# Stick-breaking attention: score banks in a ring of three pieces, turned weights in a ring of four

## What is computed

```python
def sb_attend(q, q_pos, k, v, k_pos):
    z = einsum('bqhd,bkhd->bhqk', q, k) * (SB_HEAD_DIM ** -0.5)
    mask = (k_pos[None, :] < q_pos[:, None])[None, None]
    log_keep = where(mask, log_sigmoid(-z), 0.0)
    suffix = cumsum(log_keep, axis=3, reverse=True) - log_keep
    a = where(mask, exp(log_sigmoid(z) + suffix), 0.0)
    return einsum('bhqk,bkhd->bqhd', a, v)
```

## Time and profile before

| | |
|---|---|
| median of three runs | 3169.32 us |
| the profiled execution, its time | 3168.51 us |
| its span, first to last instruction | 3166.7 us |
| PE busy, share of the span | 2966.6 us, 94% |
| PEld | 2641.9 us, 83% |
| DVE | 1229.3 us, 39% |
| ACT | 973.0 us, 31% |
| POOL | 631.6 us, 20% |
| mean granted clock of PE | 0.975 |

### The profile page before, as it was taken

One profiled execution on the slowest core, in us unless ns is written; L12 is line 12 of the kernel. 1 busy time (PEld: TensorE's weight loads), 2 busy tenths in 40 slices (PEclk: granted clock), 3 DMA queues, 4 the chain that ended last, 5 costly groups with the idle time before them and its releaser, 6 DMA issues. The chain is left out here.

```text
span 3166.7 us, 43362 instructions
## 1 busy us (share of the span) xinstructions
PE 2966.6 (94%) x16067; PEld 2641.9 (83%) x16067; DVE 1229.3 (39%) x1881; ACT 973.0 (31%) x1875; POOL 631.6 (20%) x484
## 2 busy tenths in 40 slices
PE   7989996999999999998999898898799999999998
PEld 6778885788899988997988677777679998899987
DVE  5556651432233322334111265667333332233324
ACT  4344443231122111223222365656322221122212
POOL 3100000121122111211212144444112211122111
PEclk9989997999999999999999999999899999999999
DMA  4211103310111111111355553633401111111111
GB/s 145 79 43 40 41 29 122 135 47 27 39 53 53 40 27 39 53 40 69 122 158 178 167 126 86 135 93 71 142 7 54 53 46 33 38 41 53 46 34 73
DMA packets 216172, 227.81 MB, mean 72 GB/s; under 512 B 50688, under 2 KB 174080, under 8 KB 216064
## 3 DMA queue, kind: packets, MB, share of 16 engines
q1 hardware_dynamic: 216064, 226.41, 24.3%
HBM read 170.36 MB, written 56.00 MB: 71 GB/s over the span
## 5 line engine op out<-in xcount | busy, mean ns | idle before, releaser
L1449 DVE TENSOR_TENSOR x<-m_ps,x 128x512 f32<-128x512 f32 x324 | 224.1, 692 | 669.7 <-PE m_ps L76 669.7
L1484 DVE TENSOR_TENSOR m_sq<-m_relu 128x384 f32<-128x384 f32 x192 | 171.9, 895 | 526.4 <-ACT m_relu L1388 526.4
L74 PE MATMUL m_ps<-h_h,m_up0h 128*128 128x384 f32 x768 | 259.0, 337 | 8.1 <-POOL m_up0l L1422 8.1
L75 PE MATMUL m_ps<-h_l,m_up0h 128*128 128x384 f32 x768 | 258.5, 337 | 0.0
L76 PE MATMUL m_ps<-h_h,m_up0l 128*128 128x384 f32 x768 | 258.5, 337 | 0.0
L74 PE MATMUL m_ps<-h_h,m_up1h 128*128 128x384 f32 x768 | 256.5, 334 | 0.0
L75 PE MATMUL m_ps<-h_l,m_up1h 128*128 128x384 f32 x768 | 256.5, 334 | 0.0
L76 PE MATMUL m_ps<-h_h,m_up1l 128*128 128x384 f32 x768 | 256.5, 334 | 0.0
L1388 ACT ACTIVATE m_relu<-m_ps 128x384 f32<-128x384 f32 x192 | 94.6, 492 | 515.8 <-PE m_ps L76 515.7
L2170 POOL TENSOR_TENSOR e_b<-e_b,e_r 128x128 f32<-128x128 f32 (+7 forms) x128 | 155.1, 1216 | 235.5 <-DVE e_r L2216 228.1
L2216 DVE TENSOR_TENSOR_SCAN e_r<-e_ps,e_zero 128x128 f32<-128x128 f32 (+7 forms) x128 | 173.1, 1352 | 49.8 <-ACT e_ps L2083 43.0
(11 more groups left out here) (510 smaller groups left out, 7612.6 us busy)
## 6 DMA issues: line engine op xcount, KB each, us to landing
m_up_raw<-in_mlp_w_up SPq DMA_DIRECT2D x64, 512.0 KB, 4.6
m_dn_raw<-in_mlp_w_down SPq DMA_DIRECT2D x64, 512.0 KB, 3.6
h_raw<-scratch_oT SPq DMA_DIRECT2D x4, 1536.0 KB, 15.8
scratch_qr<-a_qrst SPq DMA_DIRECT2D x9, 512.0 KB, 3.4
a_x<-in_x_prompt SPq DMA_DIRECT2D x8, 512.0 KB, 4.8
b_qr<-scratch_qr SPq DMA_DIRECT2D x4, 1024.0 KB, 6.6
scratch_oT<-b_o SPq DMA_DIRECT2D x32, 128.0 KB, 1.7
new_p_sb_k<-d_rows SPq DMA_DIRECT2D x16, 256.0 KB, 2.0
```

What stands on the lines that cost most here:

```text
L74: pe.matmul(out, w[0], m[0], start=start, stop=False)
L75: pe.matmul(out, w[0], m[1], start=False, stop=False)
L1449: dve.tensor_tensor(x[:, t, cols], bank[:, 4 + n % 3, :], x[:, t, cols], ALU.add).then_inc(added.sem, 1)
L1484: dve.tensor_tensor(sq[n % 2][:], relu[n % 2][:], relu[n % 2][:], ALU.mult).then_inc(sq_done.sem, 1)
```

## The change

Scores, sigmoids and scan of a step go by pieces of at most one bank. `chunks` gives a step's pieces, the one with the last keys first: one piece up to 512 keys; for 640 keys 256 and then 384, for 768 keys 256 and 512, for 896 keys 384 and 512, for 1024 keys 512 and 512. Banks 0 to 2 hold the pieces in a ring of three, so a piece waits for the scan of the piece three before it. The scan of a second piece starts from the last value of the first, which it waits for. Semaphores `e_s`, `e_kept`, `e_taken` and `e_scan` count pieces where they counted steps. POOL's product still covers a whole step. The bank set free goes to the transposes and the sample: their ring has four banks, 3 to 6.

```diff
--- before.py
+++ after.py
@@ -1874,6 +1874,19 @@
         return n // SbSchedule.PAIR_STEPS % 2, m // 2 % 2, 2 * (m // 4) + m % 2
 
     @classmethod
+    def chunks(cls, n):
+
+
+        keys = max((cls.where(n)[2] + 1) * P, 2 * P)
+        ends = [0, keys - 2 * P if keys == 5 * P else 4 * P, keys] if keys > 4 * P else [0, keys]
+        return [(a, b - a) for a, b in zip(ends, ends[1:])][::-1]
+
+    @classmethod
+    def chunks_before(cls, n):
+
+        return sum(len(cls.chunks(m)) for m in range(n))
+
+    @classmethod
     def sample_task(cls, n):
 
         if n % 2 == 0:
@@ -1958,12 +1971,12 @@
         wT = sb("e_wT", [P, 2, P])
         o_smp = sb("e_osmp", [P, S.PAIRS, DEC_BATCH, DEC_SEQ])
         bank = ctx.enter_context(nc.psum_tensor("e_ps", [P, 8, 512], F32))
-        score = [bank[:, 2 * u:2 * u + 2, :].rearrange("p b c -> p (b c)") for u in range(2)]
+        CHUNKS = S.chunks_before(S.STEPS)
 
         qk_in, v_in = signal("e_qk_in"), signal("e_v_in")
         s_done = signal("e_s")
         kept, taken = signal("e_kept"), signal("e_taken")
-        scanned, weighted = signal("e_scan", 2), signal("e_weighted", 2)
+        scanned, weighted = signal("e_scan", 3), signal("e_weighted", 2)
         t_done, t_hi, t_lo = signal("e_t"), signal("e_t_hi"), signal("e_t_lo", 3)
         pv_done, o_done = signal("e_pv", 2), signal("e_o", 1)
         ck_in, cv_in = signal("e_ck_in"), signal("e_cv_in")
@@ -1974,13 +1987,19 @@
         const_done = signal("e_const")
         o_out = [signal(f"e_o_out{u}", 16) for u in range(2)]
 
+        def pieces(n):
+
+            used = (S.where(n)[2] + 1) * P
+            c = S.chunks_before(n)
+            return [(c + j, key, min(width, used - key), bank[:, (c + j) % 3, 0:width])
+                    for j, (key, width) in enumerate(S.chunks(n))]
+
         def slot(m):
 
-            m %= TASKS
-            return m % 3 if m < TASKS - 1 else 1
+            return m % 4
 
         def task_bank(m):
-            return bank[:, 4 + slot(m), :]
+            return bank[:, 3 + slot(m), :]
 
         def emptied(pe, i, m):
 
@@ -2045,7 +2064,7 @@
                             load_cache_v(i, 1, 2 * i + 1)
                         if g == 0 and not (last and pair == 1):
 
-                            s_done.wait(sp, S.STEPS * i + S.PAIR_STEPS * pair)
+                            s_done.wait(sp, CHUNKS * i + CHUNKS // 2 * pair)
                             load_queries_keys(sp, scratch, operands[1 - pair], 2 * i + pair + 1, qk_in.sem)
                             pv_done.wait(sp, S.UNITS * i + S.UNITS // 2 * pair)
                             load_values(sp, scratch, operands[1 - pair], 2 * i + pair + 1, v_in.sem)
@@ -2073,14 +2092,14 @@
 
             def weights(i, n):
 
-                first, _, used = score_columns(S.where(n)[2])
-                z = score[n % 2][:, first:first + used]
-                s_done.wait(act, S.STEPS * i + n + 1)
                 if n >= 4:
 
                     t_done.wait(act, TASKS * i + S.before(n - 3))
-                act.activation(take[n % 4][:, 0:used], z, ACT.Sigmoid, scale=SB_SCALE).then_inc(taken.sem, 1)
-                act.activation(z, z, ACT.Sigmoid, scale=-SB_SCALE).then_inc(kept.sem, 1)
+                for c, key, used, z in pieces(n):
+                    s_done.wait(act, CHUNKS * i + c + 1)
+                    act.activation(take[n % 4][:, key:key + used], z[:, 0:used], ACT.Sigmoid,
+                                   scale=SB_SCALE).then_inc(taken.sem, 1)
+                    act.activation(z[:, 0:used], z[:, 0:used], ACT.Sigmoid, scale=-SB_SCALE).then_inc(kept.sem, 1)
 
             def sample(i, kind, f, ps):
                 if kind == "keys":
@@ -2164,8 +2183,8 @@
             def weigh(i, n):
 
                 used = (S.where(n)[2] + 1) * P
-                scanned.wait(pool, S.STEPS * i + n + 1)
-                taken.wait(pool, S.STEPS * i + n + 1)
+                scanned.wait(pool, CHUNKS * i + S.chunks_before(n + 1))
+                taken.wait(pool, CHUNKS * i + S.chunks_before(n + 1))
                 b = take[n % 4][:, 0:used]
                 pool.tensor_tensor(b, b, rest[n % 2][:, SEQ - used + 1:SEQ + 1], ALU.mult).then_inc(
                     weighted.sem, 1)
@@ -2209,13 +2228,17 @@
             const_done.wait(dve, 12)
 
             def scan(i, n):
-                first, _, used = score_columns(S.where(n)[2])
-                keep = score[n % 2][:, first:first + used]
-                kept.wait(dve, S.STEPS * i + n + 1)
+                total = (S.where(n)[2] + 1) * P
                 weighted.wait(dve, S.STEPS * i + n - 1)
-                dve.tensor_tensor_scan(rest[n % 2][:, SEQ - used:SEQ][:, ::-1], keep[:, ::-1],
-                                       zero[:].broadcast_to([P, used]), 1.0, ALU.mult, ALU.add).then_inc(
-                                           scanned.sem, 1)
+                for c, key, used, keep in pieces(n):
+                    kept.wait(dve, CHUNKS * i + c + 1)
+                    at, start = SEQ - total + key, 1.0
+                    if key + used < total:
+                        scanned.wait(dve, CHUNKS * i + c)
+                        start = rest[n % 2][:, at + used:at + used + 1]
+                    dve.tensor_tensor_scan(rest[n % 2][:, at:at + used][:, ::-1], keep[:, 0:used][:, ::-1],
+                                           zero[:].broadcast_to([P, used]), start, ALU.mult, ALU.add).then_inc(
+                                               scanned.sem, 1)
 
             def scan_sample(i, f):
                 kept_s.wait(dve, S.SAMPLE_STEPS * i + f + 1)
@@ -2270,16 +2293,16 @@
                 pair, a, q = S.where(n)
                 if n % S.PAIR_STEPS == 0:
                     qk_in.wait(pe, 16 * QK_LOADS * (2 * i + n // S.PAIR_STEPS + 1))
-                scanned.wait(pe, S.STEPS * i + n - 1)
-                first, chunks, used = score_columns(q)
-                for at, width, key in chunks:
+                for c, key, used, z in pieces(n):
+                    scanned.wait(pe, CHUNKS * i + c - 2)
+                    masked = key + used == (q + 1) * P
                     for k in k_tt[pair]:
-                        pe.matmul(score[n % 2][:, at:at + width], q_st[pair][:, a, q * P:(q + 1) * P],
-                                  k[:, a, key:key + width], start=k is k_tt[pair][0],
-                                  stop=k is k_tt[pair][1] and key + width < used)
-                end = first + used
-                pe.matmul(score[n % 2][:, end - P:end], io["ident16"][:], io["causal_mask"][:, 0:P],
-                          start=False, stop=True).then_inc(s_done.sem, 1)
+                        last = pe.matmul(z, q_st[pair][:, a, q * P:(q + 1) * P], k[:, a, key:key + z.shape[1]],
+                                         start=k is k_tt[pair][0], stop=k is k_tt[pair][1] and not masked)
+                    if masked:
+                        last = pe.matmul(z[:, used - P:used], io["ident16"][:], io["causal_mask"][:, 0:P],
+                                         start=False, stop=True)
+                    last.then_inc(s_done.sem, 1)
 
             def sample_keys(i, f, ps):
                 ck_in.wait(pe, 16 * (batch(i, f) + 1))
```

## The result

The changed kernel takes 3202.0 us in the median of four runs (3200.0 to 3205.5), the kernel before 3170.2 (3167.8 to 3171.5): a ratio of 1.0098, 95% interval 1.0085 to 1.0111. That is 31.8 us slower, where 3187 was forecast, with 3168 to 3208 as the range. In the code after, the scores matmul is L2300, the transposes L2356, the scan L2239, the sigmoids L2100 and L2102.

The account below looks back on a forecast made before the run. PE was taken to set the pace of the attention stage (busy 371.9 of 425 us), though not full. The terms +36 - 11 - 3 - 3 = +19 us gave 3187 us, range 3168 to 3208.

Parts of the forecast that it names:

- The chain at even steps (+36): Second score pieces at n = 10, 12, 14 of a head pair wait for the previous step's first scan: +36 us.
- T(5) to T(6): Start of step 5's transposes to step 6's in a head pair; forecast 3.1 us, before 1.72 or 1.11.
- The credits together (-17): Gains from the new rings set against the loss: -11 scan waits, -3 transposes' bank, -3 value products' low halves.
- What scan waits give back (-11): PE's scan waits in short steps and behind odd long steps: two thirds of 16.5 us go, -11.
- The fourth bank (-3): Transposes' waits for a bank, 3.3 us and a smaller sister row: a fourth turned-weights bank gives -3.
- the low halves before value products (-3): Of 6.3 us PE waits before value products, -3: the low half lands while PE stands in the scores.
- The clock (0): PE's granted clock in the attention stage: no term in the sum, slower clock held only as a rival.
- rival C: Stalls bring one more slow-clock stretch of 4 us per pair: +16 us on top, 3203 us; chance 0.12.
- Split costs: Extra scans and sigmoids: 10 to 13 us on DVE, 8 on ACT, hidden; SBUF start value put at 0.
- A: Rival: scores' scan waits just go with more pieces in flight, and the transposes' wait: -15, 3154 us; chance 0.12.
- B: Rival: even steps' stall is taken back in full by odd steps and later value products: 3172 us; chance 0.14.
- D: Rival: no ring stall, but DVE carries the stage and its 13 us arrive in full: 3182 us; chance 0.06.

Follow-up runs that it names:

- split_only: Changed kernel's pieces, but score banks as before the change (two pairs by step parity, waiting for the whole scan) and turned weights in three banks; 3169.7 us.
- ring4_pieces: Changed kernel with score pieces in a ring of four banks and turned weights back in a ring of three; 3161.9 us.
- second_piece_later: Changed kernel with PE writing the second score piece after the transposes of the step, no longer ahead of them; 3160.7 us.
- early4: Changed kernel with sigmoids, scan and POOL's product four steps ahead of the transposes, not three, with five take buffers and a small sixth; 3231.5 us.
- ring3_ring3: Changed kernel with turned weights in a ring of three banks again, one bank left unused; 3209.4 us.
- early4_values_output_later: early4 with value products one step later and ACT's output copy behind the high parts of the step; 3127.6 us.
- values_later: Changed kernel with the value products of two steps one step later in PE's order; 3265.9 us.

## Why the prediction was right, and where its size was off

The direction, the mechanism and its price came true; the credits set against it did not, and that is why 31.8 us were measured where 17 to 19 were forecast.

- **The chain at even steps (+36).** Right in kind and size. T(5) to T(6) in the other pair:

```profile
1989.18 0.60 PE L2356 MATMUL e_ps<-ident,e_b 128*128 128x128 f32 x4
...
1992.24 0.49 PE L2356 MATMUL e_ps<-ident,e_b 128*128 128x128 f32 x3
```

  3.06 us against 3.1 worked out; n = 12 came to 3.17 (3.16), n = 14 to 4.37 (4.28). Added up from the timelines, from the first transpose of a step to that of the next, over all eight pairs:

  | kernel | T(5) to T(6), T(7) to T(8), T(9) to T(10), us | all other intervals, us |
  |---|---|---|
  | before | 50.4 | 364.6 |
  | changed kernel | 86.4 | 360.2 |
  | split_only | 50.9 | 362.9 |
  | ring4_pieces | 47.2 | 359.4 |
  | second_piece_later | 44.6 | 359.8 |
  | early4 | 50.2 | 426.8 |

  That is +36.0 us for the change. It goes away with a fourth bank, with ACT's order (and its take buffer), and with PE's order; in early4 it comes back, and more, in other intervals.
- **The credits together (-17).** This is the term that was mis-sized: the stage grew by 30.1 us, so all that lies outside these three intervals gave back 6, not 17. The next three points part it.
- **What scan waits give back (-11).** Held, as waits: the even steps have 44.0 of the 57.9 us, so 13.9 are left where 24.8 were. The two at the loop's turn stayed, at 3.29 and 3.15.
- **The fourth bank (-3) and the low halves before value products (-3).** Together they gave nothing. Beside the rows, the kernel before has

```profile
PE e_ps L74 <- DVE e_pt0l L2248: 4.8, 10, 0.6
PE e_ps L2333 <- DVE e_pt1l L2248: 1.9, 4, 0.7
```

  so its waits for low halves were 11.1 us before value products and 5.2 before transposes, 16.3 in all. In the changed kernel they are 16.8 and 0.4, 17.2 in all: +0.9 where -6 was forecast. The bank let the transposes through, and the value products behind them waited for the same low halves; ring3_ring3 has the waits back in their old places, 8.6 and 8.2. The prediction names this ("what follows waits for the same low half anyhow") and still takes both credits.
- **The clock (0).** Held as a rival and left out of the sum. The stage's granted clock went from 0.94 to 0.92. Taken as a share of time at the lower level, that is 0.12 x 429 = 52 us before and 0.16 x 459 = 74 after; half of the 22 is at most 11 us of work lost. The terms above leave 26.0 of the 30.1 us, so some 4 are left over. Counted the other way, PE's idle time grew by 22.7 us and its busy time, for the same matmuls, by 7.4. Some 4 to 7 us may then be the clock's, a quarter to a half of what rival C gave for it; no run changed the clock alone.
- **Split costs.** Hidden, as said: split_only is even with the kernel before. DVE's 15.9 us lie above the 10 to 13 given; the start value read from SBUF, put at 0, is 64 x 0.06 = 3.8 of them.
- Rivals A, B and D fell: the even intervals grew, and the span with them, and split_only, which has the same 64 extra scans, isn't slower. A's rule was half right. The Trainium skill (Perfetto Trace Analysis, Optimization Strategy) ties a recurring gap to too little PSUM, and here a fourth bank did take the scan waits from 57.9 to 11.7 us. But second_piece_later took the loss back with three banks, by PE's order alone, and early4_values_output_later, with more take buffers but three score banks, has 9.3 us of scan waits left.

## What to carry to other kernels

Count a ring in steps of the loop, not in slots: three banks of one piece are one and a half steps where two pieces make a step, and that was less than the two steps of before. When a buffer gets tighter, look for the place in the producer's own order with nothing between two uses, follow the release back through every engine's queue to the same producer, and price that loop. Put work that starts the next link of such a loop ahead of the wait, and where one engine is made to run ahead, move the consumers of its results too: moved alone, the stall reappeared at the next consumer (early4). When counting what a buffer gives back, add up the waits of all who wait for the same thing: the fourth bank took 4.8 us from the transposes and put 5.7 on the value products. And measure each combination: the edit that gained 41 us in the changed kernel cost 20 us in the fastest one.

## What the runs showed of the hardware

A scan whose start value is read from SBUF takes 0.06 us longer than one with a constant: 1283 against 1224 ns for 512 columns. From the kernel after, groups by form:

```profile
L2239 DVE TENSOR_TENSOR_SCAN e_r<-e_ps,e_r,e_zero 128x512 f32<-128x512 f32 x48 | 61.6, 1283 | 8.2 <-ACT e_ps L2102 5.3
L2239 DVE TENSOR_TENSOR_SCAN e_r<-e_ps,e_zero 128x512 f32<-128x512 f32 x32 | 39.2, 1224 | 18.2 <-ACT e_ps L2102 17.5
```

Kernels with many short stalls had a lower granted clock over the whole stage: 0.94 in the kernel before, 0.83 in values_later, whose longest scan wait was 3.5 us and which had 58 of them. By the working above (0.34 of 518 us on the lower level, half of it lost) that is up to 88 us, against 26 in the kernel before: at most some 62 of the 88.5 us by which its stage is longer. PE's busy time for the same 2544 matmuls, which also holds latency behind waits, grew by 49.6 us (376.6 to 426.2), its idle time by 38.9. The rows show the clock and the stalls only as going together; no run changed the clock alone.
